# Delta rule: the 128-row inverse as two diagonal blocks of 64 on 64x64 tiles, and one block apart

## The chip, the core and the metric

The kernel runs on one core of a Trainium2 chip. The metric is the device time of one execution in microseconds, start to end; the span of a profile is from its first to its last instruction. TensorE is PE in the profile (PEld its weight loads), VectorE is DVE, ScalarE is ACT, GpSimd is POOL, SyncE is SP.

## What is computed

Two model blocks over 256 tokens of width 1024. The first has a gated delta rule (4 heads of 128) beside a dilated attention, an output projection and a feed-forward net; the second has two layers of attention, each with a mixture of 16 experts, all modulated by a vector `c`. The change is in the delta rule alone. Its core, per head and chunk of tokens:

```python
decay = jnp.exp(jnp.where(causal, g[..., :, None] - g[..., None, :], -jnp.inf))
a = jnp.where(strict, jnp.einsum('bhnik,bhnjk->bhnij', k_beta, k) * decay, 0.0)
rhs = jnp.concatenate([v * beta, k_beta * jnp.exp(g)[..., None]], axis=-1)
sol = lax.linalg.triangular_solve(a, rhs, left_side=True, lower=True, unit_diagonal=True)
...
def step(state, inp):
    v_new = uc - jnp.einsum('bhik,bhkv->bhiv', wc, state)
    o = jnp.einsum('bhik,bhkv->bhiv', qd, state) + jnp.einsum('bhij,bhjv->bhiv', aqk, v_new)
    state = state * dl[..., None, None] + jnp.einsum('bhik,bhiv->bhkv', kd, v_new)
    return state, o
```

The reference cuts the 256 tokens into chunks of 64. The kernel takes two chunks of 128 and forms the inverse of I + a (unit lower triangular) by doubling: the inverse of the blocks of size b on the diagonal gives that of the blocks of size 2b. The sizes b are 1, 2, 4, 8, 16, 32 and 64.

## The kernel before

All is float32. The four heads stand beside each other in the free dimension, so a tile of a chunk `c` is 128 partitions by 4 x 128, and a product of two of them is four matmuls into one PSUM bank of 512 columns. A float32 matmul leaves two records in the profile.

The tiles of chunk `c`: `ab[c]` is the matrix a, `mb[c]` the part of it that a level brings in (a times the mask `lev(n)` of the constants), `xm[c]` the inverse so far and `ym[c]` its transpose. Level 0 (b = 1) needs no product: `xm` is the identity less `mb` (line 2265), `ym` the identity less its transpose by PE (lines 1692 and 2267). Each level n from 1 to 6 (PE's loop at line 1709) then does:

1. PE: `mb` by `ym` for chunk 0, then chunk 1 (line 1715, into bank 3c).
2. PE: `ada`, one bundle of another work: eight records of the modulation of the second block (line 481), whose weights come by DMA.
3. ACT copies the products to `nm[c]` (line 1993), beside step 2.
4. PE: for each chunk `xm` by `nm` (line 1723) and `nm` by `xm` (line 1726), into banks 3c+1 and 3c+2.
5. PE: another `ada` bundle. Beside it DVE subtracts the products from `ym` and `xm` (lines 2301 and 2302), and earlier in the level has made the next `mb` (line 2298).

The order on each engine is written out by hand, with counted semaphores between them. At levels 3 and 4 ACT and DVE also split two weights of the output projection each (lines 520 and 524, called through `splits`), and SP then loads the next ones (line 446). At level 5 ACT first copies a finished column set of the modulation (line 1946), loads a table and applies Silu to `zs` (line 1988), and only then makes its two copies.

After level 6 the inverse is used (`heads`, line 1735): `ym[0]` by `bv[0]`, and, by way of the state between the chunks, `ym[1]` by `r1`; four more `ada` bundles stand between these products. Lines 2305 to 2328 of DVE finish the output, which PE turns (line 683) ahead of the output projection (line 534). Ahead of level 1 PE waits for the modulation's fourth group and turns a column set by sixteen tiny matmuls (line 1701).

The weights of the modulation are 1 MB for each bundle, loaded by POOL as two DMAs (line 467) into one of three places; a place is loaded again when PE has used it. POOL's first load waits for the fourth weight of the input projection; ahead of it stand two small clears (lines 1528 and 1529). `qkv_t`, `kdec`, `aqk`, `bv`, `dec` and `dect` are further tiles of the delta rule; `dec` holds the decay and `v0`, `s1`, `r1`, `v1` are names of tiles used again at the end.

Of the kernel before, what the change touches and what calls it, by code (L numbers as in the profile page):

```python
# [56 lines left out]
LEVELS = [1, 2, 4, 8, 16, 32, 64]  # L57
LAMBDA_INIT = 0.2
# [6 lines left out]
C_DIST = C_LEV + 128 * len(LEVELS)  # L65
# [83 lines left out]
def constants():  # L149
# [5 lines left out]
    for n, b in enumerate(LEVELS):  # L155

        m = (i[:, None] // (2 * b) == i[None, :] // (2 * b)) & (i[:, None] % (2 * b) >= b) & (i[None, :] % (2 * b) < b)
        c[:, C_LEV + n * P:C_LEV + (n + 1) * P] = m
# [26 lines left out]
def build_program(nc, a, out):  # L185
    ctx = ExitStack()
    with ctx:
# [65 lines left out]
        def wk(at, *shape):  # L253
            return view(work, at, shape)
# [17 lines left out]
        mb = [wk(11300 + c * 512, GDN_H, P) for c in range(2)]  # L272

        sq_t = wk(2048, 8, S)
        nm = [wk(2048 + c * 512, GDN_H, P) for c in range(2)]
# [1293 lines left out]
        def _(pe):  # L1569
# [139 lines left out]
            for n in range(1, len(LEVELS)):  # L1709
                for c in range(2):  # L1710
                    b0 = 3 * c
                    pe.wait_ge(mb_done, 2 * (n - 1) + c + 1)
                    pe.wait_ge(xy_done, 2 * (2 * (n - 1) + c + 1))
                    for h in range(GDN_H):
                        mm = nc.tensor.matmul(psum[b0][:, h * P:(h + 1) * P], mb[c][:, h, :], ym[c][:, h, :],  # L1715
                                              start=True, stop=True)
                    mm.then_inc(n_ps, 1)
                ada(31 + 2 * n)
                for c in range(2):
                    b0 = 3 * c  # L1720
                    pe.wait_ge(n_copied, 2 * (n - 1) + c + 1)
                    for h in range(GDN_H):
                        mm = nc.tensor.matmul(psum[b0 + 1][:, h * P:(h + 1) * P], xm[c][:, h, :], nm[c][:, h, :],  # L1723
                                              start=True, stop=True)
                    for h in range(GDN_H):
                        mm = nc.tensor.matmul(psum[b0 + 2][:, h * P:(h + 1) * P], nm[c][:, h, :], xm[c][:, h, :],  # L1726
                                              start=True, stop=True)
                    mm.then_inc(xyn_ps, 1)
                ada(32 + 2 * n)

            lv = 2 * (len(LEVELS) - 1)
# [835 lines left out]
```

## Time and profile before

| | us |
|---|---|
| median of 3 runs | 1262.27 (1260.25 to 1263.25) |
| the profiled execution | 1263.72 |
| its span | 1261.8 |
| busy in the span: PE | 1141.0 (90%) |
| DVE | 606.7 (48%) |
| ACT | 441.7 (35%) |
| POOL | 69.1 (5%) |
| mean granted clock of PE | 0.972 |

Busy time says on what an engine worked, not what set the end: for that there is the chain, followed back from the last instruction to what released it at each step. "issue" in it is time in which the engine waited for nothing that the profile shows. In the timelines a line merges equal records of an engine that overlap or adjoin: its start, the time to the end of the last, the count. Matmuls are pipelined, so that the length of one is longer than the distance to the next.

### The profile page before, as it was taken

The page shows a single profiled execution, that of the slowest core. Times are in us where ns is not written, and L with a number is a line of the kernel's source. Part 1 is how long each engine was busy: PE and PEld are TensorE (multiplying, and loading weights), DVE is VectorE, ACT ScalarE, POOL GpSimd, SP SyncE. Part 2 cuts the span into 40 slices and gives each one's busy share as a digit, 9 for nine tenths or more (in the row PEclk, how much of TensorE's full clock was granted, in tenths as well). Part 3 has the DMA queues.
Part 4 walks back from the last instruction along what each step waited for, and adds up shares of the span by engine and source line. Part 5 has one row for each costly group of instructions (what it writes and reads, how often), then busy time and mean ns, then how long its engine had stood idle before and what let it go on. Part 6 is the DMA issues. An engine that isn't in the chain of part 4 may idle for free.

```text
span 1261.8 us, 16821 instructions
## 1 busy us (share of the span) xinstructions
PE 1141.0 (90%) x6516; PEld 765.5 (61%) x6516; DVE 606.7 (48%) x1170; ACT 441.7 (35%) x770; POOL 69.1 (5%) x137
## 2 busy tenths in 40 slices
PE   5999979888999997996799999987999999999986
PEld 4677547578999995875563443323787863443422
DVE  3268456446666666647642323224773542323223
ACT  5344512236444556536340110103654640110200
POOL 2111232100000000000000000000000000000000
PEclk9899989988999999998899999999999999999999
DMA  9998897635677772573079999997576279999995
GB/s 292 361 290 264 298 351 265 240 117 165 180 229 227 221 226 70 198 266 134 34 304 405 412 413 414 414 414 301 189 244 256 71 275 413 412 412 414 414 413 209
DMA packets 162955, 354.23 MB, mean 281 GB/s; under 512 B 9912, under 2 KB 78776, under 8 KB 162752
## 3 DMA queue, kind: packets, MB, share of 16 engines
q1 hardware_dynamic: 146864, 296.04, 64.2%
q0 software_dynamic: 16000, 57.16, 12.9%
q8 instruction: 49, 0.80, 0.3%
q14 instruction: 26, 0.21, 0.0%
q10 hardware_dynamic: 16, 0.02, 0.0%
HBM read 352.12 MB, written 7.36 MB: 285 GB/s over the span
## 4 chain that ended last, share of the span: by engine, by line
PE 72%; DMA 14%; DVE 9%; ACT 3%; issue 1%; POOL 0%; SPq 0%; ACTq 0%; DVEq 0%
PE bank L534 35%; PE bank L1066 12%; DMA ering<-in_moe_w_up 9%; PE bank L1077 8%; DMA ering<-in_ada_w 3%; PE bank L481 3%; PE bank L1034 3%; DMA wraw<-in_w_in 2%; PE bank L683 1%; PE bank L816 1%; DVE wlo L524 1%; PE bank L1723 1%; PE bank L1715 1%; PE bank L1726 1%; PE bank L1138 1%
## 5 line engine op out<-in xcount | busy, mean ns | idle before, releaser
L524 DVE TENSOR_TENSOR wlo<-wraw,whi 128x1024 fp32r<-128x1024 f32 x150 | 179.6, 1222 | 73.9 <-ACT whi L520 71.7
L520 ACT ACTIVATE whi<-wraw 128x1024 fp32r<-128x1024 f32 x150 | 153.9, 1054 | 75.2 <-PE bank L534 54.1
L534 PE MATMUL bank<-a_hi,whi 128*128 128x256 f32 x512 | 148.7, 290 | 3.2 <-DVE wlo L524 2.1
L534 PE MATMUL bank<-a_lo,whi 128*128 128x256 f32 x512 | 146.5, 286 | 0.0
L534 PE MATMUL bank<-a_hi,wlo 128*128 128x256 f32 x512 | 146.4, 286 | 0.0
L1066 PE MATMUL bank<-ering,work 128*64 128x512 f32 x592 | 134.3, 596 | 11.9 <-DMA ering<-in_moe_w_up 10.5
L534 PEld LDWEIGHTS bank<-a_hi,whi 128*128 128x128 f32 x512 | 99.9, 195 | 17.6 <-issue 15.6
L1267 DVE TENSOR_TENSOR work<-work,bank 128x512 f32<-128x512 f32 x16 | 11.0, 687 | 206.4 <-PE bank L1066 206.4
L534 PE MATMUL bank<-whi,a_hi 128*128 128x512 f32 x256 | 102.1, 399 | 2.7 <-DVE a_lo L737 2.7
L1066 PEld LDWEIGHTS bank<-ering,work 128*64 128x64 f32 x592 | 41.1, 137 | 102.7 <-issue 78.7
L1175 ACT ACTIVATE o_hi<-work 128x512 fp32r<-128x512 f32 x32 | 20.2, 630 | 236.0 <-DVE work L1235 235.5
L534 PEld LDWEIGHTS bank<-a_lo,whi 128*128 128x128 f32 x512 | 100.0, 195 | 0.7
L534 PE MATMUL bank<-wlo,a_hi 128*128 128x512 f32 x256 | 100.2, 391 | 0.0
L534 PE MATMUL bank<-whi,a_lo 128*128 128x512 f32 x256 | 100.1, 391 | 0.0
L534 PEld LDWEIGHTS bank<-a_hi,wlo 128*128 128x128 f32 x512 | 99.8, 195 | 0.0
L1077 PE MATMUL bank<-ering,work 128*64 128x512 f32 x352 | 78.5, 595 | 1.1 <-DVE work L1270 1.1
L1235 DVE SCALAR_TENSOR_TENSOR work<-bank,sm,mrow 128x512 f32<-128x512 f32 x32 | 22.6, 747 | 91.6 <-PE bank L1077 91.6
L534 PEld LDWEIGHTS bank<-whi,a_hi 128*128 128x128 f32 x256 | 48.4, 189 | 16.3 <-issue 5.9
L1163 ACT ACTIVATE work<-bank,mcol 128x256 f32<-128x256 f32 x64 | 31.6, 561 | 68.6 <-PE bank L1034 68.6
L481 PE MATMUL bank<-ering,silc 128*32 128x512 f32 x320 | 44.1, 628 | 12.8 <-DMA ering<-in_ada_w 12.8
L534 PEld LDWEIGHTS bank<-whi,a_lo 128*128 128x128 f32 x256 | 48.3, 189 | 10.2
L534 PEld LDWEIGHTS bank<-wlo,a_hi 128*128 128x128 f32 x256 | 48.4, 189 | 9.8 <-issue 0.2
(305 smaller groups left out, 1869.8 us busy)
## 6 DMA issues: line engine op xcount, KB each, us to landing
ering<-in_moe_w_down SPq DMA_DIRECT2D x44, 1024.0 KB, 18.3
ering<-in_moe_w_up SPq DMA_DIRECT2D x42, 1024.0 KB, 18.2
ering<-in_ada_w POOLq DMA_DIRECT2D x80, 512.0 KB, 6.0
ering<-in_moe_w_gate SPq DMA_DIRECT2D x32, 1024.0 KB, 18.2
work<-in_moe_w_gate SPq DMA_DIRECT2D x16, 1024.0 KB, 16.5
wraw<-in_w_in SPq DMA_DIRECT2D x28, 512.0 KB, 8.1
wraw<-in_a_w_qkv SPq DMA_DIRECT2D x24, 512.0 KB, 4.7
work<-in_moe_w_down SPq DMA_DIRECT2D x12, 1024.0 KB, 18.4
```

What stands on the lines that cost most here:

```text
L481: mm = nc.tensor.matmul(psum[ADA_BANK][32 * q:32 * q + 32, :], silc[:, k, :], ada_at[slot][q // 2][:, (q % 2) * HALF:(q % 2 + 1) * HALF], ...
L520: nc.scalar.activation(w_hi(c), wraw[:, c % RING, :], ACT.Copy).then_inc(w_hi_done, 1)
L524: nc.vector.tensor_tensor(w_lo(u[0]), wraw[:, u[0] % RING, :], w_hi(u[0]).bitcast(F32), ALU.subtract).then_inc(w_lo_done, 1)
L534: mm = nc.tensor.matmul(out_ap, l, r, start=first and n == 0, stop=last and n == len(terms) - 1)
L683: tr = nc.tensor.transpose(turn_bank(turn, b)[:, (2 * kk + t) * P:(2 * kk + t + 1) * P], src[:, t, cols(2 * b + kk)], ident)
L816: tr = nc.tensor.transpose(psum[4 + n % 2][:, b * P:(b + 1) * P], scr[:, slot, b * P:(b + 1) * P], ident)
L1034: mm = nc.tensor.matmul(bank[:, kk * S:kk * S + cols], part[:, t, pair_cols(2 * b + kk)], sel[:, t, 0:cols // PAIR_SLOTS, :], start=n == 1 ...
L1066: mm = nc.tensor.matmul(bank[rows, :], x_e[:, k, rows], w[:, e, kk * HALF:(kk + 1) * HALF], start=first and kk == 0, stop=last and kk == 1)
L1077: mm = nc.tensor.matmul(psum[4 + half][rows, :], hid_t[:, m % 4, rows], w[:, e, half * HALF:(half + 1) * HALF], start=first, stop=last)
L1163: ins = nc.scalar.activation(xe[:, :, k, :], gather_bank(g, b)[:, kk * S:(kk + 1) * S].rearrange("p (a c) -> p a c", a=2), ACT.Identity, b ...
L1175: nc.scalar.activation(o_hi[:, cols], o_f[:, cols], ACT.Copy).then_inc(e_o_hi, 1)
L1235: return nc.vector.scalar_tensor_tensor(out=o_f[:, cols], in0=psum[4 + half][:, :], scalar=sm[:, M_GS:M_GS + 1], in1=mrow[:, 1, cols], op0 ...
```

## The change

The two diagonal blocks of 64 of a chunk's matrix (rows and columns 0 to 63, and 64 to 127) now stand below each other: the block of partitions 0 to 63 and that of partitions 64 to 127 both in columns 0 to 63 of a head. So `xm`, `ym`, `ab`, `mb` and `nm` have half the width, 4 x 64. The block left below the diagonal goes into a tile of its own, `a21`, in partitions 64 to 127.

- Levels 1 to 5: a product of a chunk is eight matmuls of 64x64 (four heads, two blocks; `blocks`), the blocks in turn, into the first 256 columns of the same banks. ACT's and DVE's work has half the columns.
- The last level forms the missing block alone: `a21` by the lower block of `y_all` and then `xm`'s upper block by that, four matmuls of 64x64 for each. `xm` isn't updated and its product is left out. DVE writes the block, negated, into `y_all`.
- `y_all[c]` is the full transposed inverse of 128 x 4 x 128 that the closing products read. POOL clears both at its start (two memsets ahead of its first wait). Level 5 writes its two diagonal blocks, with two DVE instructions instead of one.
- Ahead of level 1, `ab` is written by two instructions and `a21` by a third, and the first transpose is eight matmuls against the identity's blocks instead of four transposes.
- The masks in the constants have 64 columns each, the last is left out, and a stacked identity of 64 columns is added.

```diff
-        xm = [wk(12324 + c * 512, GDN_H, P) for c in range(2)]
-        ym = [wk(13348 + c * 512, GDN_H, P) for c in range(2)]
-        ab = [wk(9252 + c * 512, GDN_H, P) for c in range(2)]
+        xm = [wk(12324 + c * 512, GDN_H, 64) for c in range(2)]
+        ym = [wk(12580 + c * 512, GDN_H, 64) for c in range(2)]
+        y_all = [wk(13348 + c * 512, GDN_H, P) for c in range(2)]
+        ab = [wk(9252 + c * 512, GDN_H, 64) for c in range(2)]
+        a21 = [wk(9508 + c * 512, GDN_H, 64) for c in range(2)]
...
+            for c in range(2):
+                nc.gpsimd.memset(y_all[c], 0.0).then_inc(pads_zero, 1)
...
                 for h in range(GDN_H):
-                    tr = nc.tensor.transpose(psum[c][:, h * P:(h + 1) * P], mb[c][:, h, :], ident)
+                    for r in BLOCKS:
+                        tr = nc.tensor.matmul(psum[c][r, h * 64:(h + 1) * 64], mb[c][r, h, :], ident[r, r], start=True, stop=True)
                 tr.then_inc(m1_ps, 1)
...
+            def blocks(bank, l, r_):
+
+                for h in range(GDN_H):
+                    for r in BLOCKS:
+                        mm = nc.tensor.matmul(bank[r, h * 64:(h + 1) * 64], l[r, h, :], r_[r, h, :], start=True, stop=True)
+                return mm
+
+            for n in range(1, LAST):
                 for c in range(2):
-                    b0 = 3 * c
                     pe.wait_ge(mb_done, 2 * (n - 1) + c + 1)
                     pe.wait_ge(xy_done, 2 * (2 * (n - 1) + c + 1))
-                    for h in range(GDN_H):
-                        mm = nc.tensor.matmul(psum[b0][:, h * P:(h + 1) * P], mb[c][:, h, :], ym[c][:, h, :],
-                                              start=True, stop=True)
-                    mm.then_inc(n_ps, 1)
+                    blocks(psum[3 * c], mb[c], ym[c]).then_inc(n_ps, 1)
                 ada(31 + 2 * n)
                 for c in range(2):
-                    b0 = 3 * c
                     pe.wait_ge(n_copied, 2 * (n - 1) + c + 1)
...
+                    blocks(psum[3 * c + 1], xm[c], nm[c])
+                    blocks(psum[3 * c + 2], nm[c], xm[c]).then_inc(xyn_ps, 1)
                 ada(32 + 2 * n)
 
+            lo, up = BLOCKS
+            for c in range(2):
+                pe.wait_ge(xy_done, 2 * (2 * (LAST - 1) + c + 1))
+                for h in range(GDN_H):
+                    mm = nc.tensor.matmul(psum[3 * c][lo, h * 64:(h + 1) * 64], a21[c][up, h, :], y_all[c][up, h, 64:128],
+                                          start=True, stop=True)
+                mm.then_inc(n_ps, 1)
+            ada(31 + 2 * LAST)
+            for c in range(2):
+                pe.wait_ge(n_copied, 2 * (LAST - 1) + c + 1)
+                for h in range(GDN_H):
+                    mm = nc.tensor.matmul(psum[3 * c + 1][lo, h * 64:(h + 1) * 64], xm[c][lo, h, :], nm[c][lo, h, :],
+                                          start=True, stop=True)
+                mm.then_inc(xyn_ps, 1)
+            ada(32 + 2 * LAST)
...
+                for r in BLOCKS:
+                    nc.vector.tensor_tensor(ab[c][r, :, :], by_head(c)[r, :, r], dec[c][r, :, r], ALU.mult)
+                nc.vector.tensor_tensor(a21[c][up, :, :], by_head(c)[up, :, lo], dec[c][up, :, lo], ALU.mult
+                                        ).then_inc(kk_done, 1)
...
-                    nc.vector.tensor_tensor(ym[c], ym[c], by_head(3 * c + 1), ALU.subtract).then_inc(xy_done, 1)
-                    nc.vector.tensor_tensor(xm[c], xm[c], by_head(3 * c + 2), ALU.subtract).then_inc(xy_done, 1)
+                    if n == LAST:
+                        nc.vector.tensor_scalar(y_all[c][lo, :, 64:128], by_block(3 * c + 1, lo), -1.0, None, ALU.mult
+                                                ).then_inc(xy_done, 1)
+                    elif n == LAST - 1:
+                        dve.wait_ge(pads_zero, 4)
+                        for r in BLOCKS:
+                            ins = nc.vector.tensor_tensor(y_all[c][r, :, r], ym[c][r, :, :], by_block(3 * c + 1, r),
+                                                          ALU.subtract)
+                        ins.then_inc(xy_done, 1)
+                    else:
+                        nc.vector.tensor_tensor(ym[c], ym[c], by_block(3 * c + 1), ALU.subtract).then_inc(xy_done, 1)
+                    if n < LAST:
+                        nc.vector.tensor_tensor(xm[c], xm[c], by_block(3 * c + 2), ALU.subtract).then_inc(xy_done, 1)
```

## Rows read from the trace of the kernel before

**Rows 1.** The page's chain that ended last, by line:
```profile
PE bank L534 35%; PE bank L1066 12%; DMA ering<-in_moe_w_up 9%; PE bank L1077 8%; DMA ering<-in_ada_w 3%; PE bank L481 3%; PE bank L1034 3%; DMA wraw<-in_w_in 2%; PE bank L683 1%; PE bank L816 1%; DVE wlo L524 1%; PE bank L1723 1%; PE bank L1715 1%; PE bank L1726 1%; PE bank L1138 1%
```

**Rows 2.** Chain in order of time, 187 to 238: start us, us, what:
```profile
188.01 3.56 PE bank L1715 x16
...
197.33 1.98 PE bank L1715 x16
...
201.40 0.89 PE bank L1726 x8
...
205.07 1.98 PE bank L1715 x16
...
219.56 1.04 PE bank L481 x8
...
224.28 1.16 PE bank L1723 x8
...
229.11 1.98 PE bank L1715 x16
...
235.89 0.69 DVE work L2301
...
237.23 1.16 PE bank L1735 x8
```

**Rows 3.** Windows of 5 us: busy us, granted clock, DMA share, GB/s:
```profile
185.00:190.00 5.00, 5.00 (x25) 5.00 (x25) 0.04 (x1) 0.04 (x1) 0.04 (x1) 0.50 0.82 311
190.00:195.00 5.00, 5.00 (x38) 4.00 (x38) 1.76 (x3) 1.16 (x2) 1.05 (x2) 0.86 0.18 43
```

**Rows 4.** PE timeline ahead of level 1: start us, us, work [idle before]:
```profile
177.11 1.09 PE L1692 MATMUL bank<-con,work 128*128 128x128 f32 x8
...
181.72 1.93 PE L481 MATMUL bank<-ering,silc 128*32 128x512 f32 x8 [2.05 <-DMA ering<-in_ada_w]
```

**Rows 5.** Timeline of ACT in level 5:
```profile
223.65 1.06 ACT L1993 ACTIVATE work<-bank 128x512 f32<-128x512 f32 x2
```

**Rows 6.** Lines 1726 and 1066: durations of their matmuls, ns min/median/max:
```profile
L1726 PE MATMUL bank<-work x96: 275/275/275, 193.5 to 235.6; 128*128 128x128 f32 x96
...
L1066 PE MATMUL bank<-ering,work x592: 592/592/644, 657.4 to 1237.6; 128*64 128x512 f32 x198
```

**Rows 7.** Groups by shape, whole span: busy us, mean ns, idle before:
```profile
L1066 PE MATMUL bank<-ering,work 128*64 128x512 f32 x592 | 134.3, 596 | 11.9 <-DMA ering<-in_moe_w_up 10.5
...
L1006 DVE TENSOR_TENSOR work<-work,bank 128x256 f32<-128x256 f32 x22 | 9.1, 413 | 0.0
...
L1935 ACT ACTIVATE work<-bank 128x256 f32<-128x256 f32 x12 | 4.5, 376 | 12.5 <-PE bank L534 12.5
```

**Rows 8.** Timelines of PE and PEld over four heads' scores, 957 to 959.7 us:
```profile
957.98 0.50 PE L794 MATMUL bank<-work 64*128 64x128 f32 x4 [1.27 <-ACT work L2054]
958.28 0.64 PE L795 MATMUL bank<-work 64*128 64x256 f32 x4
958.71 0.49 PE L794 MATMUL bank<-work 64*128 64x128 f32 x4
...
957.95 0.34 PEld L794 LDWEIGHTS bank<-work 64*128 64x128 f32 x4 [1.66 <-issue]
958.17 0.34 PEld L795 LDWEIGHTS bank<-work 64*128 64x128 f32 x4
...
958.82 0.19 PEld L795 LDWEIGHTS bank<-work 64*128 64x128 f32 x1
```

**Rows 9.** DMA from 190 to 248 us, GB/s in 40 slices:
```profile
GB/s 40 0 37 223 418 45 212 393 285 342 215 124 311 415 412 396 410 328 356 338 325 364 390 377 381 379 393 110 246 393 266 367 181 130 342 376 339 271 0 0
DMA packets 6134, 15.85 MB, mean 273 GB/s; under 512 B 484, under 2 KB 2532, under 8 KB 6130
```

**Rows 10.** POOL: a group by shape, then a line of its timeline:
```profile
L1560 POOL MEMSET work<- 64x512 f32 x1 | 0.5, 522 | 81.1 <-DMA work<-t_rows 81.1
...
14.54 2.27 POOL L467 DMA_DIRECT2D ering<-in_ada_w  x4 [13.63 <-DMA wraw<-in_w_in]
```

More of the change, by code:

```diff
@@ L57 @@
 LEVELS = [1, 2, 4, 8, 16, 32, 64]
+LAST = len(LEVELS) - 1
+BLOCKS = [slice(0, 64), slice(64, 128)]
 LAMBDA_INIT = 0.2
@@ L64 @@
 C_LEV = 384
-C_DIST = C_LEV + 128 * len(LEVELS)
+C_EYE = C_LEV + 64 * (len(LEVELS) - 1)
+C_DIST = C_EYE + 64
 C_CNT = C_DIST + 384
@@ L154, in constants @@
     c[:, C_TRIU:C_TRIU + P] = i[:, None] <= i[None, :]
-    for n, b in enumerate(LEVELS):
+    c[:, C_EYE:C_EYE + 64] = i[:, None] % 64 == i[None, 0:64]
+    for n, b in enumerate(LEVELS[:-1]):
         m = (i[:, None] // (2 * b) == i[None, :] // (2 * b)) & (i[:, None] % (2 * b) >= b) & (i[None, :] % (2 * b) < b)
-        c[:, C_LEV + n * P:C_LEV + (n + 1) * P] = m
+        c[:, C_LEV + n * 64:C_LEV + (n + 1) * 64] = m[:, 0:64] + m[:, 64:128]
     dist = np.concatenate([i[:, None] - i[None, :], P + i[:, None] - np.arange(S)[None, :]], 1)
@@ L267, in build_program @@
         qkb = wk(10276, 8, S)
-        xm = [wk(12324 + c * 512, GDN_H, P) for c in range(2)]
-        ym = [wk(13348 + c * 512, GDN_H, P) for c in range(2)]
-        ab = [wk(9252 + c * 512, GDN_H, P) for c in range(2)]
+        xm = [wk(12324 + c * 512, GDN_H, 64) for c in range(2)]
[3 more added lines that the diff above has]
+        a21 = [wk(9508 + c * 512, GDN_H, 64) for c in range(2)]
         aqk = [wk(10276 + c * 512, GDN_H, P) for c in range(2)]
-        mb = [wk(11300 + c * 512, GDN_H, P) for c in range(2)]
+        mb = [wk(11300 + c * 512, GDN_H, 64) for c in range(2)]
         sq_t = wk(2048, 8, S)
-        nm = [wk(2048 + c * 512, GDN_H, P) for c in range(2)]
+        nm = [wk(2048 + c * 512, GDN_H, 64) for c in range(2)]
+        v0, s1 = [wk(2048 + c * 512, GDN_H, P) for c in range(2)]
         dec = [wk(3072 + c * 512, GDN_H, P) for c in range(2)]
@@ L1721, in _ @@
                     pe.wait_ge(n_copied, 2 * (n - 1) + c + 1)
[L1722 to L1727, printed above, removed]
@@ L1736, in heads @@
                 mm.then_inc(signal, 1)
-            v0, s1, r1, v1 = nm[0], nm[1], dec[0], dec[1]
-            pe.wait_ge(xy_done, 2 * (lv + 2))
+            r1, v1 = dec[0], dec[1]
+            pe.wait_ge(xy_done, 4 * LAST + 2)
             pe.wait_ge(modc_done, 2)
-            heads(psum[6], lambda h: ym[0][:, h, :], lambda h: bv[0][:, h, :], fin_ps)
+            heads(psum[6], lambda h: y_all[0][:, h, :], lambda h: bv[0][:, h, :], fin_ps)
             ada(45)
@@ L1751, in _ @@
             pe.wait_ge(fin_r, 1)
-            heads(psum[3], lambda h: ym[1][:, h, :], lambda h: r1[:, h, :], fin_ps)
+            heads(psum[3], lambda h: y_all[1][:, h, :], lambda h: r1[:, h, :], fin_ps)
             ada(48)
@@ L2246, in _, with by_block @@
             nc.vector.tensor_tensor(kdec, by_head(4), bc(M_EKL, 4, P), ALU.mult).then_inc(vtr_done, 1)
-            lev = lambda n: con[:, C_LEV + n * P:C_LEV + (n + 1) * P].unsqueeze(1).to_broadcast([P, GDN_H, P])
+            lev = lambda n: con[:, C_LEV + n * 64:C_LEV + (n + 1) * 64].unsqueeze(1).to_broadcast([P, GDN_H, 64])
+            lo, up = BLOCKS
+            def by_block(bank, rows=slice(0, P)):
+                return psum[bank][rows, 0:S].rearrange("p (a b) -> p a b", a=4)
             for c in range(2):
```

17 lines of the change are left out of this document (7 added, 10 removed).

## The prediction

> **What bounds the kernel now.** I read the page first: by lines, the chain that ended last is TensorE (PE) work in many small pieces, with the inverse's three lines (1715, 1723, 1726) among them at 1% each, some 38 us together [rows 1]. So I went to the chain in order of time over the stage of the inverse, from 188.0 to 237.2 us [rows 2]. There it is nearly all PE: a level is 1.98 us of L1715 (8 products, two records each), a bundle of the modulation (L481) of 1.0, four groups of L1723 or L1726 (0.89 each, 8 records, the first 0.2 more) and another bundle, 7.74 us from 197.33 to 205.07. A record is 0.89 / 8 = 111 ns; the 0.2 comes once behind each bundle, as L1715's 1.98 for twice 0.89 shows. ScalarE's and VectorE's copies lie beside this. Three exceptions: level 1 starts with the clock at half (granted 0.50, then 0.86) [rows 3]; level 5 waits for ScalarE (220.68 to 224.28) [rows 2, 5]; and after level 6 PE waits 1.3 us for VectorE's two subtractions [rows 2]. Ahead of the stage PE waits for a modulation weight (2.05 us to 181.72), and behind that for its copy and L1701's tiny matmuls, until 188.0 [rows 2, 4]; the change touches none of these.
>
> So what a record of a 64x64 tile costs decides, and everything behind the stage follows PE: the saving goes through to the end.
>
> **The record's price.** Call p the time from one record to the next where the two diagonal blocks alternate. A level has 48 records now, and 96 of half the columns after (2 chunks, 4 heads, 2 blocks, 2 records, for three products). The trace has no 64x64 tile, so I bound p.
> - A record alone: a matmul of 512 columns lasts 592 ns, one of 128 lasts 275 [rows 6]: 0.826 ns a column, so 64 columns fewer give 111 - 53 = 58 ns. With no overlap of the blocks p is 58.
> - Overlap by column tiles: 592 records of L1066 (half the array's columns, 512 wide) take 134.3 us, 227 each [rows 7], where one alone would be 111 + 317 = 428. The factor is 0.53.
> - Overlap by row tiles: scores of heads whose rows lie at 0 and 64. Eight records start at 957.98 and the next eight at 958.71 [rows 8]; by columns alone they would take 4 x 111 + 4 x 217 = 1312 ns. The factor is 0.56. Their weight loads overlap too: four take 0.34 us and one alone 0.19, so that they start 0.15 / 3 = 50 ns apart, though each loads 128 columns. With 0.56, p is 58 x 0.56 = 32.
> - Issue: in that burst eight loads and five matmuls start from 957.95 to 958.32, 28 ns an instruction, 57 for a pair of load and matmul [rows 8]. That is the densest that I found and no proven limit; now a pair takes 111.
> Bounds below 58 are 32 and above it 111, where each record costs what it does today. I take 50: nearest to the densest burst, a little under it because nothing shows that the burst was at a limit, and well above 32 because two instructions in 32 ns are seen nowhere.
>
> **The sum**, against the profiled execution (1263.72 us, span 1261.8):
> - Level 1: its first product runs cold; 32 records at some 80 ns (half of 107 at the cold clock plus the same extra) are 2.6 for 3.56. The bundle behind it then falls into the slow clock, which I let return at the same time, 191.4: it costs 1.4 for 1.0. The second part is 64 x 50 + 0.2 = 3.4 for 3.77. Together -0.9.
> - Levels 2 to 4: 32 x 50 + 0.2 = 1.8, bundle 1.0, 3.4, bundle 1.0 make 7.2 for 7.74; three of them -1.6.
> - Level 5: from the bundle's end at 220.60 ScalarE copies a column set, loads a table, does two Silus and then the copy that PE waits for. That copy halves (376 ns for 128x256 [rows 7]), 3.5 for 3.68; with 3.4 and 1.0 the level is 7.9 for 8.51: -0.6.
> - Level 6: one block only, on one tile at 58 ns: 16 records 0.93 + 0.2, bundle 1.0, 16 records 1.13, bundle 1.0, 4.3 in all, for 8.12 (229.11 to 237.23). The negation that takes the place of the two subtractions (0.4 us for half the width) fits under the last bundle. -3.8.
> The sum is -6.9. Taken off the median of 1262.27, which is 1.45 below the profiled run, it gives 1255.4.
>
> **At nothing.** VectorE's masks and subtractions go from 0.69 to 0.41 us (413 ns for 128x256 [rows 7]), and the two split writes in level 5 add one of these; without the cover of the second half of the products and a bundle (2.6 us at p = 50) a chunk would wait up to 1.3 us. The a21 and block copies before level 1 add 0.5 us a chunk to VectorE, the sixteen matmuls for the first transpose replace 8 records of 1.09 us [rows 4] by 32 of 1.6 us; both end before the weight that PE awaits at 181.72, with 2 us to spare, and before L1715 at 188.0. Uncovered the transposes would cost 0.5. POOL's two clears of 128x512 (522 ns for 64x512 [rows 10], so 1 us) come ahead of its first wait, which ends at 14.54 us; nothing is queued behind them until then. The smaller constants are a shorter load, not waited for.
> - Modulation weights: POOL reloads a place when PE has used it, so a faster PE asks sooner. From 190 to 248 us 15.85 MB move, with nothing in the first 3 us and the last 3 (slices of 1.45 us) [rows 9]; at the 415 GB/s or so of the best slices they need 38 of those 52 us, and 45 are left at p = 50. So it stays hidden there, with little room in levels 3 and 4, where the output projection's units load too; it caps the gain at some 14 us. With no cover (every bundle loading only once the last is used) each of 12 bundles would cost the 1.5 us by which a megabyte at that rate (2.5) outlasts its own 1.0.
>
> **The rivals.** The slope is 480 records (five levels), 0.48 us per ns of p.
> - Full overlap, p 32 to 40: -11.7 to -14, the latter being the cap of the weights: 1248 to 1250.5. For it: both factors in the trace. Against: the pair rate. 0.15.
> - Forecast, p 41 to 57: 1251 to 1258.8. 0.43.
> - No overlap: the two blocks write different partitions of one bank, while the heads of rows 8 write different banks and the column tiles of L1066 share their rows. If one bank takes one row tile at a time, p is 58 to 63 and a level is no faster; only level 6 pays: -3.1 to -0.7, 1259.2 to 1261.6. The Trainium skill ("TensorEngine Tiling (Array Packing)", Restrictions and Gotchas) states this rule: "Different row tiles cannot access same PSUM bank simultaneously." By that rule the time would be the 1259.2 to 1261.6 just worked out, by the forecast's overlap 1255; no row of this trace shows two row tiles in one bank. 0.17.
> - Slower: twice as many instructions, each load and matmul pair with a fixed cost. From p = 64.5 on the extra records eat what level 6 gives; at 75 it is 12 - 6.9 = +5.1, 1267.4; at 111 +22.4, 1284.7. For it: pairs under 57 ns are nowhere in the trace, and the tile alternates at every second record. Against: the loads 50 ns apart. 0.18.
> - The clock: PE is held at half by low activity before 191 [rows 3], though L1701's tiny matmuls keep it busy for the whole of the first window. If small tiles count as little, a level costs 96 x 80 ns + two bundles of 1.93 [rows 4] + 0.4, some 12 us for 7.74: four such levels +17, the first and fifth some 6 more, level 6 down to 7.0 for 8.12, so +22 near 1284. 0.07.
>
> **How the numbers follow.** Faster by over 0.2% means under 1259.7, slower over 1264.8 (about what a measurement of this kernel can tell from no change). Forecast and full overlap are faster, and a little of the third case: 0.62. The third case's rest and p up to 70 are the same: 0.15. The rest of the fourth and the clock are slower: 0.23. The range leaves out the very bottom, the clock and p over 77: 1248 to 1268.
>
> **What would show it.** In the chain of the changed kernel, 32 records of the first product in 1.6 + 0.2 us and 64 in 3.2 + 0.2 in level 2; 58 ns a record and a level of 4.3 us at the last; no wait for VectorE ahead of the closing products, which now start at 237.23 and then near 230.3; the wait for ScalarE in level 5 larger by 0.2 to 0.7; no idle PE before L481 for a weight. The forecast is wrong if p isn't between 41 and 57, if the granted clock isn't 1.00 from 192 on, or if a wait for a modulation weight stands between levels.

## The result, and the profile after

| | before | after |
|---|---|---|
| median of 11 runs each, us | 1262.27 (1256.21 to 1264.98) | 1254.7 (1250.76 to 1257.1) |
| the profiled execution, us | 1263.72 | 1255.5 |
| its span, us | 1261.8 | 1253.7 |
| mean granted clock of PE | 0.972 | 0.968 |

The ratio is 0.9938, interval 0.9925 to 0.9952: 7.8 us faster (7.6 by the medians). The forecast was 1255.4. The total is hit, but by luck: two terms of the sum that led to it were far off, in opposite directions, and a third effect was not in it.

The changed kernel's lines have moved: the modulation's bundle L481 is now L490, L1701's tiny matmuls are L1713, the first transpose L1692 is L1704, ScalarE's copy L1993 is L2017, the products of levels 1 to 5 (L1715, L1723, L1726 before) are all L1725, the last level is L1744 and L1751, the closing products L1735 are L1758, the turn L683 is L692, and POOL's weight load L467 is L476.

The changed kernel's chain in order of time, over the inverse (start us, us, what; against [rows 2]):
```profile
184.33 3.47 PE bank L1713 x16
187.81 1.90 PE bank L1725 x32
...
191.47 2.01 PE bank L1725 x64
...
196.60 0.28 issue
196.88 0.52 POOL ering L476
197.40 7.07 DMA ering<-in_ada_w
...
206.43 9.67 DMA ering<-in_ada_w
...
218.14 8.48 DMA ering<-in_ada_w
...
228.59 2.01 PE bank L1758 x8
```
In [rows 2] this stretch is PE but for 3.7 us of ScalarE in level 5 and 1.3 of VectorE at the end. Here the chain leaves PE at 196.60, in level 2, and from there to 226.6 it is three times the same: a bundle is used, POOL reloads its place, and 7 to 10 us later the weight lands that a later bundle waits for. The waits themselves stand in PE's timeline of the changed kernel (start us, us, work, [idle before, and who ended it]):
```profile
194.41 1.15 PE L1725 MATMUL bank<-work 64*64 64x64 f32 x32
195.49 1.06 PE L490 MATMUL bank<-ering,silc 128*32 128x512 f32 x8
196.49 2.08 PE L1725 MATMUL bank<-work 64*64 64x64 f32 x64
...
204.51 1.06 PE L490 MATMUL bank<-ering,silc 128*32 128x512 f32 x8 [0.69 <-DMA ering<-in_ada_w]
...
209.90 1.06 PE L490 MATMUL bank<-a_raw,silc 128*32 128x512 f32 x8 [3.24 <-DMA a_raw<-in_ada_w]
...
217.63 2.08 PE L1725 MATMUL bank<-work 64*64 64x64 f32 x64 [0.33 <-ACT work L2017]
...
223.76 1.06 PE L490 MATMUL bank<-ering,silc 128*32 128x512 f32 x8 [1.53 <-DMA ering<-in_ada_w]
```
Level 2 runs without a wait: 64 records (matmuls of 64x64) start at 196.49 and what follows starts at 198.50, 2.01 us; 32 take 1.08. By the difference a record costs (2.01 - 1.08) / 32 = 29 ns. From level 3 on PE runs out of weights: with three more (1.03, 0.38 and 0.42) the waits for them are 7.3 us in all.

Windows of the changed kernel, one for each of levels 2 to 6, then one over the end of level 6 and the start of the closing products (us; busy us and count of PE, PEld, DVE, ACT, POOL; granted clock, DMA share, GB/s):
```profile
194.48:199.56 5.08, 5.08 (x115) 3.27 (x116) 2.72 (x9) 2.66 (x4) 2.10 (x4) 1.00 1.01 356
199.56:205.57 6.01, 5.21 (x115) 3.26 (x115) 5.21 (x9) 2.66 (x4) 2.09 (x4) 1.00 0.97 329
205.57:214.12 8.55, 5.23 (x116) 3.27 (x116) 3.49 (x8) 0.77 (x2) 2.09 (x4) 1.00 1.03 403
214.12:221.15 7.03, 5.29 (x114) 3.29 (x114) 2.23 (x6) 3.58 (x6) 2.09 (x4) 1.00 1.06 378
221.15:228.59 7.44, 5.49 (x51) 2.66 (x49) 1.03 (x3) 0.76 (x2) 2.09 (x4) 0.78 1.03 384
225.00:230.00 5.00, 4.58 (x31) 2.73 (x30) 0.83 (x2) 0.00 (x0) 2.09 (x4) 0.54 1.01 382
```
A level is 5.1 us of PE's work, where it was 7.74 [rows 2], but takes up to 8.55. The stage of the inverse took 49.22 us (188.01 to 237.23 [rows 2]) and takes 40.78 (187.81 to 228.59). PE's busy time in it fell by more, from 48.10 to 32.97 us (6.67 in the first level, and the rows of levels 2 to 6 above), so that of the 15.1 us that PE saved, 8.4 reached the stage and 6.7 became idle time in it.

Of those 8.4 some were lost again: the clock, at 1.00 from level 2 to level 5, falls in level 6 and is 0.54 in the window from 225 to 230. From the first closing product to the turn it is 18.3 us (228.59 to 246.90), 16.65 before (237.23 to 253.88): +1.7. With the stage's start (0.2 earlier) the turn starts 7.0 us earlier. The spans end 8.1 apart; the 1.1 between is made in places that the change doesn't touch, and of a size that single executions scatter by (see e4).

DMA from 190 to 235 us of the changed kernel (GB/s in 40 slices; against [rows 9]):
```profile
GB/s 80 15 44 211 401 360 309 346 310 291 382 317 328 379 404 404 419 412 410 399 400 342 341 380 397 381 396 392 389 403 377 393 375 364 411 310 251 295 353 197
DMA packets 5903, 15.04 MB, mean 334 GB/s; under 512 B 456, under 2 KB 2504, under 8 KB 5897
...
ering<-in_ada_w POOLq DMA_DIRECT2D x16, 512.0 KB, 6.9
```
Nothing is left of the gaps in [rows 9] (45, 124, 110, 130 GB/s) but the one at the start: while PE does L1713 and the first level's products, no place comes free. From the fourth slice on the rate is (334 x 40 - 139) / 37 = 357 GB/s on the mean, with the share at 1.0.

### The profile page after: what moved, and what is told of

It is laid out like the page before. It is cut to its first block, busy times and chain, and to the rows that moved or that the text cites. A ratio compares the mean times of both kernels' runs of the same rounds, so it can differ in the third digit from the quotient of the medians.

```text
span 1253.7 us, 17321 instructions
## 1 busy us (share of the span) xinstructions
PE 1128.0 (90%) x6764; PEld 752.0 (60%) x6764; DVE 595.9 (48%) x1172; ACT 438.9 (35%) x770; POOL 70.1 (6%) x139
## 4 chain that ended last, share of the span: by engine, by line
PE 72%; DMA 14%; DVE 8%; ACT 3%; issue 1%; POOL 0%; SPq 0%; ACTq 0%; DVEq 0%
PE bank L543 37%; PE bank L1075 12%; DMA ering<-in_moe_w_up 9%; PE bank L1086 7%; DMA ering<-in_ada_w 5%; PE bank L490 3%; PE bank L1043 3%; PE bank L825 1%; PE bank L692 1%; DVE wlo L533 1%; PE bank L1147 1%; PE bank L804 1%; PE bank L803 1%; PE bank L1758 1%; ACT hn L634 1%
## 5 line engine op out<-in xcount | busy, mean ns | idle before, releaser
L529 ACT ACTIVATE whi<-wraw 128x1024 fp32r<-128x1024 f32 x150 | 153.9, 1054 | 75.2 <-PE bank L543 54.1
L543 PEld LDWEIGHTS bank<-a_hi,whi 128*128 128x128 f32 x512 | 100.2, 196 | 17.1 <-issue 15.1
L490 PE MATMUL bank<-ering,silc 128*32 128x512 f32 x320 | 44.0, 627 | 16.8 <-DMA ering<-in_ada_w 16.6
L543 PEld LDWEIGHTS bank<-whi,a_lo 128*128 128x128 f32 x256 | 48.3, 189 | 10.2
## 6 DMA issues: line engine op xcount, KB each, us to landing
ering<-in_moe_w_down SPq DMA_DIRECT2D x44, 1024.0 KB, 18.3
work<-in_moe_w_down SPq DMA_DIRECT2D x12, 1024.0 KB, 18.3
```

The lines of the kernel that those rows point to most:

```text
L490: mm = nc.tensor.matmul(psum[ADA_BANK][32 * q:32 * q + 32, :], silc[:, k, :], ada_at[slot][q // 2][:, (q % 2) * HALF:(q % 2 + 1) * HALF], ...
L529: nc.scalar.activation(w_hi(c), wraw[:, c % RING, :], ACT.Copy).then_inc(w_hi_done, 1)
L543: mm = nc.tensor.matmul(out_ap, l, r, start=first and n == 0, stop=last and n == len(terms) - 1)
```

## The experiments

The ratios are to runs of the kernel before on the same chip. In each expectation A and B are the theories of that comparison, as it names them.

**Are the weights what holds the stage?** Two kernels load half the columns of every bundle from number 35 on (counted from 0; the level 2 bundle at 198.50 in the changed kernel), so that half of these weights is left out. One is built on the kernel after and one on that before:
```diff
-                nc.gpsimd.dma_start(ada_at[slot][h], a["ada_w_2"][l][k * P:(k + 1) * P, j * D:(j + 1) * D]
+                w_ = D if n < 35 else D // 2
+                nc.gpsimd.dma_start(ada_at[slot][h][:, 0:w_], a["ada_w_2"][l][k * P:(k + 1) * P, j * D:j * D + w_]
```


> The changed kernel, but of the modulation's weights only half is loaded from bundle 35 on (the first 512 columns of each part, 0.5 MB for 1 MB; the second half keeps what the place held, so that this part of the modulation isn't computed). Matmuls are the same. Theory A, after the change the arrival of these weights sets the levels: no wait for a weight between levels is left, levels 3 and 4 take 5.1 us like level 2, level 5 some 6.6, level 6 some 4.3, the clock stays at 1.00 in the closing products; 8 to 9.5 us faster than the changed kernel, ratio to the kernel before 0.986 to 0.988. Theory B, the waits only take up slack that something else would fill (ScalarE's and VectorE's copies between the products): under 3 us faster, ratio above 0.991.

Measured: 1244.69 us (4 runs), ratio 0.9856 [0.9833, 0.9879]. The ratio is theory A's, a little lower. Two waits for weights are left in the levels (0.67 and 0.50 us, where A had none), the stage is 33.84 us (188.59 to 222.43), and the clock is 1.00 from level 2 to the last closing product. e2's PE timeline (its lines are one higher), the last level and the first closing product:
```profile
218.00 1.44 PE L1745 MATMUL bank<-work 64*64 64x64 f32 x16
...
220.37 1.14 PE L1752 MATMUL bank<-work 64*64 64x64 f32 x16
221.44 1.06 PE L491 MATMUL bank<-ering,silc 128*32 128x512 f32 x8
222.43 1.16 PE L1759 MATMUL bank<-work 128*128 128x128 f32 x8
```


> The kernel before with the same halved loads from bundle 35 on (half of each part isn't computed). Theory A, in the kernel before the weights hide behind PE: no difference beyond 1.5 us, ratio 0.999 to 1.001. Theory B, contention of these loads already costs the kernel before something (the output projection's units, level 5): 3 us or more faster, ratio under 0.998.

Measured: 1261.02 us (10 runs), ratio 0.9991 [0.9975, 1.0007]: nothing, as theory A had it. So the loads cost the old kernel nothing that can be measured and the new one some 10 us (1254.7 against 1244.69 by the medians; 0.9938 - 0.9856 of 1262 is the same). That is shown. Its place is shown for 7.8 us of it: the turn starts at 239.08 in e2's trace and at 246.90 in after's. The two profiled executions are 6.6 us apart (1248.89, the slowest of e2's four, and 1255.5). The last level without them takes 4.4 us (218.00 to 222.43), for which the prediction had 4.3, and its L1752 gives the price of a record on a single tile at full clock: 16 in 1.07 us, of which 0.15 is the start, so 57.5 ns (predicted 58).

**How far do two tiles overlap, and does the order matter?** Three orders of the same products.
```diff
-                for h in range(GDN_H):
-                    for r in BLOCKS:
+                for r in BLOCKS:
+                    for h in range(GDN_H):
```


> The changed kernel with the matmuls of levels 1 to 5 in another order: the four heads of the upper block first, then the four of the lower one, where the changed kernel takes the two blocks in turn. Instructions and results are the same. Theory A, the records are cheap because two blocks run beside each other: with seven of eight neighbours on the same tile a record costs 56 to 60 ns again, a level some 8.0 us of PE (32 and 64 records, 0.4, two bundles), levels 1 to 6 some 46 us instead of 40.8, and the closing products again at full clock; 3 to 5 us slower than the changed kernel, ratio to the kernel before 0.996 to 0.998. Theory B, a 64x64 tile costs 28 ns a record by itself: no difference from the changed kernel, ratio 0.994.

Measured: 1256.72 us (5 runs), ratio 0.9941 [0.9918, 0.9965]. e1's PE timeline in level 2:
```profile
194.75 1.54 PE L1725 MATMUL bank<-work 64*64 64x64 f32 x32
196.22 1.06 PE L490 MATMUL bank<-ering,silc 128*32 128x512 f32 x8
197.22 2.69 PE L1725 MATMUL bank<-work 64*64 64x64 f32 x64
199.84 1.07 PE L490 MATMUL bank<-a_raw,silc 128*32 128x512 f32 x8
```
32 records take 1.47 us and 64 take 2.62: 36 ns by the difference, and 0.3 us at each start. Runs of eight records on one tile still overlap, though less. Neither theory had this price (56 to 60, or 28); the ratio is theory B's, but not for its reason. Each level is a microsecond longer in PE than after's (6.1 against 5.1), and yet the stage is 41.8 us (185.98 to 227.81) against 40.8: the longer work fills what the weights leave idle.

e7 does both products of levels' second half on the upper block, then both on the lower, 16 records on a tile at a time:
```diff
-                    blocks(psum[3 * c + 1], xm[c], nm[c])
-                    blocks(psum[3 * c + 2], nm[c], xm[c]).then_inc(xyn_ps, 1)
+                    for r in BLOCKS:
+                        for bank, l, r_ in ((psum[3 * c + 1], xm[c], nm[c]), (psum[3 * c + 2], nm[c], xm[c])):
+                            for h in range(GDN_H):
+                                mm = nc.tensor.matmul(bank[r, h * 64:(h + 1) * 64], l[r, h, :], r_[r, h, :], start=True, stop=True)
+                    mm.then_inc(xyn_ps, 1)
```


> The changed kernel; in the second part of a level both products of the upper block come first (16 records on one tile) and then both of the lower. Alternating blocks gave 29 ns a record, runs of eight 36 (e1_order), one tile alone 57.5 in the last level. Theory A, a tile can run ahead of the other by a few records only: with runs of 16 the 64 records cost 45 to 52 ns each, 3.0 to 3.4 us. Theory B, the engine looks ahead far enough to fill both tiles whatever the order, and the 36 are only restarts between groups: 32 to 38 ns, 2.1 to 2.5 us.

Measured: 1261.59 us (1 run). e7's PE timeline in level 2:
```profile
198.96 3.40 PE L1739 MATMUL bank<-work 64*64 64x64 f32 x64
202.29 1.07 PE L490 MATMUL bank<-a_raw,silc 128*32 128x512 f32 x8
```
64 records in 3.33 us: (3.33 - 0.15) / 64 = 50 ns, as theory A had it. Not all of the total is from this price: the clock falls in level 5, and level 6 runs at half.

e8 issues the upper block's matmul twice and leaves the lower block out, so that all records fall on one tile:
```diff
-                    for r in BLOCKS:
+                    for r in (BLOCKS[0], BLOCKS[0]):
```


> The changed kernel, but in levels 1 to 5 the upper block's matmul is issued twice and the lower block isn't computed: the same number of records of the same size, all on one tile. Theory A, the 29 ns are two tiles beside each other: a record costs 56 to 60 ns, the 64 of a second part 3.7 to 4.0 us, a level some 8 us. Theory B, a small record is cheap by itself: 29 ns as in the changed kernel, 2.0 us.

Measured: 1290.5 us (1 run). e8's PE timeline in level 3:
```profile
204.81 7.09 PE L1725 MATMUL bank<-work 64*64 64x64 f32 x64
211.83 1.08 PE L490 MATMUL bank<-a_raw,silc 128*32 128x512 f32 x4
```
and windows of e8 (columns as above):
```profile
185.00:190.00 5.00, 5.00 (x41) 3.68 (x40) 0.85 (x2) 0.77 (x2) 0.00 (x0) 0.50 0.35 139
...
240.00:245.00 5.00, 5.00 (x38) 3.22 (x37) 0.75 (x2) 2.39 (x3) 1.04 (x2) 0.50 0.19 39
```
64 records in 7.02 us are 110 ns, 55 at full clock: no overlap on one tile, as with L1752 above and as theory A had it. And the clock stays at half through all levels with PE busy all the time.

Together, at full clock: 29 ns where the tile changes at each matmul (two records), 36 with eight records on a tile, 50 with sixteen, 57.5 on one tile. Against 57.5 each, a run of eight saves 8 x 21 = 170 ns and one of sixteen 16 x 7.5 = 120, two to three records; a run of two saves 57, one of its two records, which is all that two tiles can. So it looks as if two or three records at each change of tile run beside those of the other tile, whatever the length of the run. This reading is worked out from the sizes; no run shows the queue behind it.

**What is the last level's unneeded product worth?** The kernel before, without L1726's product and the subtraction from `xm` in its last level, which nothing reads:
```diff
-                    for h in range(GDN_H):
-                        mm = nc.tensor.matmul(psum[b0 + 2][:, h * P:(h + 1) * P], nm[c][:, h, :], xm[c][:, h, :],
+                    if n < len(LEVELS) - 1:
+                        for h in range(GDN_H):
+                            mm = nc.tensor.matmul(psum[b0 + 2][:, h * P:(h + 1) * P], nm[c][:, h, :], xm[c][:, h, :],
...
-            pe.wait_ge(xy_done, 2 * (lv + 2))
+            pe.wait_ge(xy_done, 2 * (lv + 2) - 2)
```


> The kernel before with 128x128 tiles, in which only the last level leaves out the product into xm (line 1726) and its subtraction, whose result nothing reads. Theory A, the last level lies on the path in full: 16 records of 111 ns (1.8 us) and VectorE's last subtraction (0.6) go, 2.4 us faster, ratio 0.998. Theory B, something else sets the start of the closing products: no difference, ratio 1.000.

Measured: 1263.2 us (12 runs), ratio 1.0011 [0.9995, 1.0027]: no gain in the total; the expectation fails. e4's chain behind the stage:
```profile
235.06 1.09 PE bank L1736 x8
...
238.00 6.73 DMA a_raw<-in_ada_w
...
252.29 3.68 PE bank L683 x16
```
a window of e4:
```profile
494.00:498.00 4.00, 4.00 (x10) 3.13 (x11) 3.35 (x7) 2.54 (x5) 0.00 (x0) 0.50 0.00 0
```
and the same window of the kernel before:
```profile
494.00:498.00 4.00, 2.63 (x19) 2.24 (x18) 3.83 (x8) 2.04 (x4) 0.00 (x0) 1.00 0.00 0
```
The closing products start 2.2 us earlier (237.23 in [rows 2]). The last bundle then waits for its weight (loaded from 238.00, landed at 244.7), and the turn is 1.6 us earlier. Some 240 us later the clock is at half in e4 and at full in before, on the same work (L534's products; the windows hold different parts of it, as e4 is 3.0 us ahead there). The first twelve of them start over 4.73 us in e4 (493.79 to 498.52) and over 2.61 in before (496.82 to 499.43), so this costs it 2.1 us. So a place like this one, where PE comes back from a wait, can move a single execution by 2 us, which is more than the turn had gained. Whether that happens in the median of 12, or something else ate the 1.6 us, these runs don't tell.

**Can the weights be given more room?** Five kernels put the bundles in other places. In the code `ada(k)` issues every bundle up to the k-th that isn't done yet. e5, on the kernel after, leaves eight bundles in the levels (33 to 40) for twelve, puts four between the closing products (41 to 44) and four (45 to 48, the last `ada(48)`) behind them, where PE waited 5.37 us for VectorE:
```diff
+AFTER_FIRST = [32, 33, 35, 36, 37, 38, 39]
+AFTER_SECOND = [32, 34, 35, 37, 38, 39, 40]
...
-                ada(31 + 2 * n)
+                ada(AFTER_FIRST[n])
...
-                ada(32 + 2 * n)
+                ada(AFTER_SECOND[n])
...
-            ada(45)
+            ada(41)
...
-            ada(48)
+            ada(44)
             pe.wait_ge(fin_copied, 3)
             heads(psum[4], lambda h: aqk[1][:, h, :], lambda h: v1[:, h, :], fin_ps)
+            ada(48)
```
ScalarE's copies of the modulation's columns move behind the work that the levels and the closing products wait for. The two moves were not tried apart.

> The changed kernel with the sixteen modulation bundles of the stage set elsewhere: two each in levels 1 and 3, one each in levels 2, 4, 5 and 6 (behind the products except in level 2), four between the closing products as before, and four behind them, where PE waits for VectorE and no transfer runs. ScalarE's column copies move with them. All work is the same. Theory A, the arrival of the weights is what the 64x64 tiles run into: eight bundles instead of twelve are due by the closing products, these start near 216.5 us for 228.6, the four late bundles fit into the 5.4 us gap, and the clock stays at 1.00 for the turn behind it; the turn starts near 234 us for 246.9, 12 to 16 us faster than the changed kernel, ratio to the kernel before 0.981 to 0.985. Theory B, with one bundle in a level the copies and subtractions of ScalarE and VectorE lie bare and take back what the weights give: less than 5 us faster than the changed kernel, ratio 0.990 or more.

Measured: 1246.88 us (4 runs), ratio 0.9883 [0.9863, 0.9903]. e5's PE timeline from the first closing product on:
```profile
216.41 1.16 PE L1760 MATMUL bank<-work 128*128 128x128 f32 x8
...
231.32 1.06 PE L492 MATMUL bank<-a_raw,silc 128*32 128x512 f32 x8 [3.01 <-DMA a_raw<-in_ada_w]
233.82 1.94 PE L492 MATMUL bank<-ering,silc 128*32 128x512 f32 x8 [1.43 <-DMA ering<-in_ada_w]
236.34 1.93 PE L492 MATMUL bank<-ering,silc 128*32 128x512 f32 x8 [0.58 <-DMA ering<-in_ada_w]
238.83 1.69 PE L492 MATMUL bank<-a_raw,silc 128*32 128x512 f32 x8 [0.56 <-DMA a_raw<-in_ada_w]
240.45 1.97 PE L694 MATMUL bank<-con,hn 128*128 128x128 f32 x16
```
The ratio lies between the two theories (0.981 to 0.985, and 0.990 or more). The closing products start 12 us earlier than after's, as A had it, but the turn only 6.5 and not 13 (1.3 of the 6.5 comes of an earlier start of the stage, 186.40 for 187.74 in PE's timelines). The last four bundles arrive 2.5 us apart and set it. The transfers, not the order of PE's work, are the bound; moving only takes out the idle stretches. This is the fastest of the kernels that compute everything, and beats both.

The same places in the kernel before:

> The kernel before, 128x128 tiles, with the bundles moved in the same way. Theory A, its levels are bound by PE: the four bundles that leave the levels give 4 us, the gap's warm clock some 2 to 3 more, ratio 0.994 to 0.996; the tiles are then worth 9 to 10 us beside e5_moved_after, more than the 7.8 of the change as it was made. Theory B, the gain of moving the bundles is the same for both kernels (12 us or more here too): ratio 0.990 or less.

Measured: 1264.08 us (12 runs), ratio 1.003 [1.0012, 1.0047], a little slower; both expectations fail. The profiled execution took 1271.24 us, the slowest of the twelve, so its trace shows more loss than the median has. e6's PE timeline:
```profile
235.83 1.16 PE L1737 MATMUL bank<-work 128*128 128x128 f32 x8 [0.38 <-DVE work L2305]
...
254.48 1.93 PE L483 MATMUL bank<-ering,silc 128*32 128x512 f32 x8 [3.39 <-DMA ering<-in_ada_w]
...
258.81 3.46 PE L685 MATMUL bank<-con,hn 128*128 128x128 f32 x15
```
The stage starts at 191.13 here by the chain, 3.1 us later than in [rows 2], and ends 1.4 earlier, so the levels gave 4.5 us. But loads only start as bundles are used, and used late they come late: the four behind the closing products wait 0.40, 1.46, 3.39 and 0.53 us, two of them then run at half clock (1.93 us), and the stretch of 5.4 us before the turn has become 11.7 (247.1 to 258.8).

e10 goes the other way and puts level 1's two bundles (33 and 34) ahead of L1713's tiny matmuls, to free two places before the levels begin; e9 does this and e5's kind of move (with other bundles in each place):
```diff
+            ada(34)
             mod_columns(psum[6])
```


> The changed kernel with one edit: the first two modulation bundles of level 1 are issued before L1713's tiny matmuls instead of inside level 1, so that POOL can reload their places some 5 us sooner; no byte and no matmul is more or less. Theory A, the weights set the stage from the first reload (191.8 us in the changed kernel, with the DMA idle from 189 to 193) to the last: the reload starts near 186, the 7.3 us of waits ahead of bundles shrink to 2 to 3, the closing products start near 224 for 228.6 and the turn behind them near 241 for 246.9; 4 to 6 us faster than the changed kernel, ratio to the kernel before 0.989 to 0.991. Theory B, PE itself sets it: level 1 only starts later by what it loses in bundles, no difference from the changed kernel, ratio 0.993 to 0.995.

Measured: 1254.14 us (11 runs), ratio 0.9942 [0.9923, 0.9961], as after and as theory B had it.

> Both edits: two bundles before L1713, none in level 1, one each behind levels 2 to 5 and in level 3's place as before, two in level 6, four between the closing products and four behind them. In e5_moved_after the four late ones came 2.5 us apart, as the weights landed, and the turn began at 240.45. Theory A, the last weight lands as much sooner as the first reload starts, 4 to 5 us: the turn near 236, ratio to the kernel before 0.984 to 0.986, 3 to 5 us faster than e5_moved_after. Theory B, the places are reloaded one by one behind PE's own pace by then, the early start is used up: the same as e5_moved_after within 1.5 us, ratio 0.987 to 0.989.

Measured: 1254.62 us (11 runs), ratio 0.9931 [0.9906, 0.9956], neither of the two. Timeline of POOL's load issues in e10:
```profile
187.95 1.04 POOL L476 DMA_DIRECT2D ering<-in_ada_w  x2 [1.11 <-PE bank L490]
197.21 1.05 POOL L476 DMA_DIRECT2D ering<-in_ada_w  x2 [8.21 <-PE bank L490]
```
and e9:
```profile
202.62 1.04 POOL L478 DMA_DIRECT2D ering<-in_ada_w  x2 [11.68 <-PE bank L492]
```
The first early bundle waits for its own weight (2.14 us at 183.54 in e10), and the gap without loads doesn't go, it moves: POOL has nothing to reload for 8.2 us in e10 and 11.7 in e9, while PE does levels without a bundle between them. Three places are all there are, so what is loaded sooner must be used sooner.

Since e5's four runs lay close together and e9's eleven did not, e5's kernel and the one after were run once more, beside each other:

> The kernel of e5_moved_after once more, beside the changed kernel on the same chip: its ratio of 0.988 rests on four runs, and e9_early_moved, which also sets four bundles behind the closing products, gave 0.993. Theory A, e5's order is truly faster, as its trace shows (turn at 240.45 us for 246.9): ratio to the kernel before 0.986 to 0.990, and 5 to 8 us under e12_after_again. Theory B, its first runs were a lucky draw of when the early weights arrive: ratio 0.991 to 0.994, within 3 us of e12_after_again.

> The changed kernel itself, for the comparison with e11_moved_again. Both theories: ratio 0.992 to 0.995 as measured; the 64 records of a second part again 2.01 us and waits ahead of bundles of some 5 to 8 us over levels 3 to 6.

Measured: the moved bundles 1248.89 us (6 runs), ratio 0.9897 [0.987, 0.9923]; after 1252.56 (8 runs), 0.9934 [0.9912, 0.9956]. The change's own ratio comes out as before. The moved bundles gain another 3.7 us here, where the first pair had 7.8 (1246.88 against 1254.7); the ratio is e11's theory A, the distance neither theory's (5 to 8, or under 3). The traces say less than 7.8: from the stage's start to the turn it is 59.2 us in after, 54.1 in e5, 58.7 in e12 and 54.8 in e11, so the moved bundles save 5.1 and 3.9. The sign holds; how much of that reaches the end is open between 4 and 8. e12's PE timeline shows after's waits again (this one, and 0.60, 1.38, 0.42 and 1.33 us beside it):
```profile
206.79 1.07 PE L490 MATMUL bank<-a_raw,silc 128*32 128x512 f32 x8 [3.53 <-DMA a_raw<-in_ada_w]
```

## Why the prediction came out right, step by step

- **What bounds the kernel: right.** The small products on PE were on the path; the turn behind them came 7.0 us earlier, and the total fell by 7.8.
- **The record's price: wrong, too high.** p was 29 ns, not 50, and below the lower bound of 32. The step that failed is the choice by the densest burst: 57 ns for a pair of load and matmul in [rows 8] was what that burst did, not what the engine can. The changed kernel does a pair in 29. The factor of 0.56 for two row tiles came near (58 x 0.56 = 32); the measured one is 29 / 57.5 = 0.50, full overlap. By the prediction's slope of 0.48 us a nanosecond this term alone makes 480 x 21 ns = 10.1 us more than the 6.9 of the sum.
- **The modulation weights at nothing: wrong.** They were said to be hidden at p = 50, and to cap the gain at some 14 us. They bound from level 3 on, and the stage gave 8.4. The cap was a sum of bytes over a rate, and the rate was the term that was mis-sized: 415 GB/s was taken from the best slices of [rows 9], and with the share at 1.0 the core moved 357 on the mean. The same sum with that rate is 15.85 MB / 357 GB/s = 44.4 of 52 us, which leaves 7.6, near the stage's 8.4. [rows 9] had it to read: the fifteen busy slices from the thirteenth on (311 to 393) are 372 GB/s on the mean, which leaves 9.4. The rate of busy stretches, not of the best slice, would have given about the cap. At p = 50 the sum would have been about at it: e1, whose PE is a microsecond a level longer, has nearly the same stage. That is why a wrong p cost the forecast nothing.
- **Levels 2 to 4**: 5.08, 6.01 and 8.55 us for 7.2 each, 19.6 for 21.6 in all; without waits 5.1 each. **Level 5**: 7.03 for 7.9. ScalarE's wait in it is 0.33, with 1.4 us for weights around it. It was 0.74 before and was to grow by 0.2 to 0.7; in e2, with 0.50 us of waiting for a weight ahead of it, it is 0.87 us.
- **Level 6: 7.44 us for 4.3**, the largest miss of a single term. Its parts are as priced (57.5 ns a record, and 4.4 us in e2), but 1.53 and 0.42 us of waits for weights are on top, and a clock of 0.78: 1.93 us in place of 1.06 for the last bundle and 1.48 in place of 1.14 for L1751, 1.2 together.
- **Level 1**: 3.66 us to the end of the first bundle (187.81 to 191.47), 4.0 predicted. The clock was back when it was before, as predicted (0.69 on the mean from 190 to 192, 0.66 before); that it is 0.74 over this level and 0.82 over the old one comes of the level's length, 6.67 us for 9.32.
- **What was put at nothing and was**: VectorE's masks and subtractions (no wait for it between levels or ahead of the closing products), the first transpose (32 records in 1.15 us from 178.45, ahead of the weight that PE awaits), POOL's memsets, ahead of its first wait.
- **Not in the sum**: the clock's fall, 1.2 us in level 6 and 1.7 in the closing products. The prediction had a rival for the clock, but all through the levels, at 1284. e8 shows that this rival is real for a single tile. With the tiles alternating it doesn't occur in levels 2 to 5. Why it falls in level 6 is not shown. Two things differ there, the 16 + 16 records on a single tile and the waits. e2 has the first and no wait in level 6, and no fall. e1 and e10 have both, the same products and waits at the same two bundles (1.41 and 0.70 us in e1, against 1.53 and 0.42 in the changed kernel), and yet the clock stays at 1.00 there. e10's PE timeline in level 6:
```profile
222.54 1.06 PE L490 MATMUL bank<-ering,silc 128*32 128x512 f32 x8 [1.73 <-DMA ering<-in_ada_w]
...
225.44 1.07 PE L490 MATMUL bank<-ering,silc 128*32 128x512 f32 x8 [0.76 <-DMA ering<-in_ada_w]
```

e7's clock falls already in level 5, behind waits of 0.21 and 1.15 us and ahead of level 6's products, and is 0.50 from 225 to 230 with PE busy all the time. So the fall comes in some executions (after, e12, e7) and not in others, and neither the single tile nor the waits is enough to bring it.

- **The rivals.** Full overlap was the right mechanism, with 0.15; its time of 1248 to 1250.5 wasn't reached, since the cap on it was too loose. No overlap within one bank is refuted: 29 ns against 57.5, in the same bank, with the tiles in different partitions of it. By the prediction's 0.826 ns a column the 64 columns of a record alone take 53 ns, so that at 29 ns two tiles' records run at the same time. The Trainium skill ("TensorEngine Tiling (Array Packing)", Restrictions and Gotchas) says "Different row tiles cannot access same PSUM bank simultaneously." The measurement decides: for two tiles that differ in rows and columns the rule doesn't hold here. Two row tiles that write the same partitions of a bank were not tried. The rival of a fixed cost for each instruction falls too: 29 ns for a load and a matmul, 14.5 an instruction. The Trainium skill ("TensorE: Matmul & The Clock Gate", "Wait — 56ns, not 53.3ns?") says that matmuls never start closer together than about 25 ns; the 29 ns here agree, and its section would have been a better lower bound than the burst of [rows 8].
- **What the prediction said would make it wrong**: all three came true, p outside 41 to 57, a clock below 1.00 behind 192, and waits for weights between levels. So the total was right by luck, by two errors that met: PE got faster than forecast by 10.1 us in the sum, and waits for weights (7.3 us) and the clock (1.2 and 1.7) took back 10.2. This is an account of one execution, with e2 and e3 as the proof of its largest part.

Still open: why the clock falls in level 6 in some executions; what of the scatter between executions is the clock's (e4) and what the DMA's; how much of the gain is the last level's alone in the changed kernel, which no run undoes there; and whether the moved bundles give 4 or 8 us.

## What to carry to other kernels

When work on the path gets cheaper, price what comes next with the mean rate of its busy stretches and not with its best slice: here the compute saved 15 us, and transfers that cost nothing before took back nearly half. Two tiles of 64x64 on the array's diagonal halve the price of small fp32 products, also within one bank, if the tile changes at every matmul; long runs on one tile lose most of it. A densest burst in a trace is what that code did; it bounds nothing from below.

## What the runs showed of the hardware that was not expected

- Two 64x64 tiles in different rows and columns of the array, writing different partitions of one bank, overlap fully: 29 ns a record against 57.5.
- The overlap depends on the order: 29, 36, 50 and 57.5 ns a record for runs of 2, 8, 16 and all records on one tile.
- Load and matmul pairs on two alternating tiles follow each other at 29 ns.
- With the levels' products all on a single tile PE stays at half clock (0.50) for over 50 us while it is busy all the time (e8); with the tiles alternating it is 1.00 in levels 2 to 5 (after).
- With three places to reload, the core's DMA moves 357 GB/s on the mean at a share of 1.0, and 329 to 403 in the windows of single levels; a load of 512 KB into `ering` lands 6.9 us after its issue (median).
- The same work near 494 to 498 us ran at clock 1.00 in one execution and 0.50 in another (before and e4), at a cost of 2.1 us.
- The same level 6, with the same kind of waits, ran at full clock in e1 and e10 and partly at half in after and e12.
